# Another order in the middle of a hybrid mixer, and its second inverse transform as eight matmuls

## Chip, cores and metric

One Trainium2 chip, one of its cores. The metric is the time of one execution on the device in microseconds (us). Engines are named as the profile names them: PE is TensorE (PEld its weight loads), DVE is VectorE, ACT is ScalarE, POOL is GpSimd, SP is SyncE.

## What is computed

A two-layer encoder on 256 tokens of width 1024, in float32. Each layer is a SwiGLU block, a mixer, and another SwiGLU block; the mixer joins three branches and projects them by one 1024 x 1024 matrix.

```python
def hybrid_layer(x, ...):
    x = x + 0.5 * swiglu_ffn(rms_norm(x, ffn1_norm), ...)
    proj = rms_norm(x, mix_norm) @ w_in
    y_hy  = hyena_mixer(hy_in, ...)          # width 256
    y_mla = mla_mixer(mla_cq, mla_ckv, mla_kr, ...)   # 4 heads, width 512
    y_gla = gla_mixer(gla_q, gla_k, gla_v, ...)       # 4 heads, width 256
    x = x + jnp.concatenate([y_hy, y_mla, y_gla], axis=-1) @ w_out
    x = x + 0.5 * swiglu_ffn(rms_norm(x, ffn2_norm), ...)
    return x

def fft_long_conv(u, kern, skip):
    L = u.shape[1]
    U = jnp.fft.rfft(u, n=2 * L, axis=1)
    K = jnp.fft.rfft(kern, n=2 * L, axis=0)
    y = jnp.fft.irfft(U * K[None], n=2 * L, axis=1)[:, :L]
    return y + u * skip.astype(jnp.float32)

def hyena_mixer(u_proj, ...):
    u = centred_short_conv(u_proj, conv_w, conv_b).astype(jnp.float32)
    v, x1, x2 = jnp.split(u, HY_ORDER + 1, axis=-1)
    z = x1 * fft_long_conv(v, kern[:, 0], skip[0])
    y = x2 * fft_long_conv(z, kern[:, 1], skip[1])
    return rms_norm(y.astype(dtype), out_norm)
```

The attention branch (MLA) computes queries from a 256-wide latent and keys and values from a 128-wide one, turns 64 dimensions of each query and of one shared key by rotary angles, and takes a softmax over 256 keys. The gated linear attention branch (GLA) computes decayed scores between all pairs of tokens.

## The kernel before

**Tiling.** Tokens are 2 tiles (T) of 128. Products with weights run as three fp32r passes over a high and a low part: ACT copies the high part of a weight slot (L409, helper `hi`), DVE subtracts it for the low part (L681, helper `lo`), and PE runs L1036 to L1038 (helper `passes`). Weights stream through a ring of three slots of 1 MB, filled by SP. Products of activations with activations or small tables run in plain float32; each such matmul stands in the trace as two MATMUL records, so the four matmuls of one inverse transform are 8 records.

**Order.** Every engine runs its own list of instructions in the order of its block in the source, with semaphores between the lists; nothing else orders the work. A `wait_ge` on an engine holds all that follows on that engine.

**The Hyena branch.** Each of the two long convolutions (o = 0 and 1) is, in turn:
- `hy_dft` on PE (L1191): four float32 matmuls, the odd positions' half into one PSUM bank, the even half into another.
- `spectrum_odd` on ACT (L518): the odd half copied to SBUF; `join` on DVE (L840): even plus odd and even minus odd, into C, which holds the spectrum at both halves of the frequencies.
- `multiply` (L853) and `combine` (L863) on DVE: the complex product with the filter's spectrum. Both inputs of their four operations lie in SBUF; the result is Y, four parts of 256 columns.
- `fold` on DVE (L869): sums and differences of Y's halves, so that the inverse needs half as many matmuls; then it signals `h_y`.
- `hy_inverse` on PE (L1202): four float32 matmuls with the table `idft`; signals `h_inv`.
- `gated` on DVE (L874): times x1 or x2; signals `h_z`.

After o = 1, ACT sums squares (L640), POOL forms the reciprocal root (`rstd`, L321 to L323), and DVE scales the two tiles of 256 columns (L980 to L984), which signals `h_yy` for PE's transposes (`turn_group(l, 2, 0, ...)`, L1357).

**The GLA branch.** It runs eight levels. For each: `level_exp` on ACT (L522), `level_qk` on DVE (L801), `levels` on POOL (L339, four additions on line L350 that prepare the next level), `level_scores` on PE (L1178, line L1187, into banks 0 to 3), and `level_keep` on DVE (L807, a predicated copy, line L815). `level_scores(l, b)` waits until `level_keep(l, b - 1)` has emptied the banks (for b = 0: until ACT's copy to AD, L635). `level_exp(l, b)` waits for POOL's `levels(l, b - 1)` and DVE's `level_qk(l, b - 1)`.

**The attention branch.** Queries come out in bank 7 (rotary part, slot S_UQR) and banks 2 and 3; DVE forms the rotary products (L963 to L965, `a_qt`), POOL adds them (L379, `a_qr`), PE transposes (L1334), ACT copies out (L628, `a_qre`), and PE computes `scores` (L1209, lines L1212 and L1213): row block s = 0 into banks 4 and 5, s = 1 into banks 6 and 7. `hy_dft(l, 1, 6)` and `hy_inverse(l, 1, 6)` also use banks 6 and 7, so scores of s = 1 come after them. `score_max` on DVE (L817) and `probs` on ACT (L536) follow.

DVE's order after the second convolution, unchanged in source: `level_qk(2)`, `level_keep(0)`, `gated(1)`, `level_qk(3)`, `score_max(0)`, `level_keep(1)`, `level_qk(4)`.

## Time and profile before

| | |
|---|---|
| time of 3 runs | 1040.04 to 1040.89 us, median 1040.7 |
| profiled execution, its own time | 1040.12 us |
| its span, first to last instruction | 1038.1 us |
| granted TensorE clock, mean | 0.999 |
| PE busy | 1010.4 us, 97% of the span |
| DVE busy | 637.3 us, 61% |
| ACT busy | 485.4 us, 47% |
| POOL busy | 111.6 us, 11% |
| mean DMA rate | 169 GB/s |

Times inside the trace are counted from the first instruction; the layers are two copies of the same lists, and the mixer's middle lies near 255 to 330 us in layer 0 and 765 to 840 us in layer 1. Of a matmul the trace knows the start; its end is modelled. Where a row has a bracket, the engine sat idle for that long before it, and what ended the idle time is named. Line numbers are those of the kernel before.

### The profile page before, as it was taken

The numbers are of one execution on the slowest core, as the hardware profiler recorded it, in microseconds if no ns is written. First come the engines' busy times: TensorE is split into PE (matmuls) and PEld (weight loads), VectorE is DVE, ScalarE is ACT, GpSimd is POOL, SyncE is SP. The second block draws the span as 40 slices with busy tenths as digits, with TensorE's granted clock in tenths as the row PEclk, the third lists the DMA queues.
The fourth block names the chain that finished last, engine by engine and source line by source line (L and its number), as shares of the span: only waits on it lengthen the run. The fifth ranks groups of instructions, "written<-read, shape, count | busy, mean of one in ns | idle before, by whom it ended". The sixth has DMA issues, their size and how long they took to land.

```text
span 1038.1 us, 17426 instructions
## 1 busy us (share of the span) xinstructions
PE 1010.4 (97%) x7004; PEld 923.8 (89%) x7004; DVE 637.3 (61%) x738; ACT 485.4 (47%) x663; POOL 111.6 (11%) x160
## 2 busy tenths in 40 slices
PE   7999999999899999999999999999998999999997
PEld 6999999888778999999999999997886889999996
DVE  4655555676886655555566555557679765555555
ACT  6544434356654544343354443434566554434342
POOL 2000000150331100000020000003315220000001
PEclk9999999999999999999999999999999999999999
DMA  9565455444303554555555545552542245455551
GB/s 306 188 227 203 167 197 181 143 163 150 135 22 142 202 202 168 197 179 184 183 178 203 203 167 197 179 185 86 199 164 80 81 148 218 167 197 178 186 182 41
DMA packets 27084, 175.93 MB, mean 169 GB/s; under 512 B 3200, under 2 KB 3712, under 8 KB 6560
## 3 DMA queue, kind: packets, MB, share of 16 engines
q1 hardware_dynamic: 25744, 172.90, 46.5%
q0 software_dynamic: 720, 1.95, 0.7%
q8 instruction: 33, 0.54, 0.2%
q10 hardware_dynamic: 576, 0.45, 0.2%
q14 instruction: 11, 0.09, 0.0%
HBM read 174.58 MB, written 1.05 MB: 169 GB/s over the span
## 4 chain that ended last, share of the span: by engine, by line
issue 50%; PE 38%; POOL 9%; DVE 1%; DMA 1%; POOLq 1%; ACT 0%; SPq 0%; DVEq 0%; ACTq 0%
PE psum L1036 13%; PE psum L1037 13%; PE psum L1038 13%; POOL mixer_scratch L350 3%; POOL mixer_scratch L371 1%; POOL mixer_scratch L370 1%; DMA x<-in_x_dram 1%; POOL statistics L323 1%; POOL statistics L321 1%; POOL statistics L334 0%; POOL x_normed L375 0%; DVE x L727 0%; POOL statistics L337 0%; POOLq L226 0%; POOL mixer_scratch L372 0%
## 5 line engine op out<-in xcount | busy, mean ns | idle before, releaser
L681 DVE TENSOR_TENSOR w_low<-w_raw,w_high 128x2048 fp32r<-128x2048 f32 (+1 forms) x160 | 362.8, 2271 | 198.5 <-ACT w_high L409 198.5
L1036 PE MATMUL psum<-xT_high,w_high 128*128 128x256 f32 x1536 | 437.8, 285 | 1.7 <-DVE xT_low L691 1.6
L1037 PE MATMUL psum<-xT_low,w_high 128*128 128x256 f32 x1536 | 435.3, 283 | 0.0
L1038 PE MATMUL psum<-xT_high,w_low 128*128 128x256 f32 x1536 | 435.2, 283 | 0.0
L409 ACT ACTIVATE w_high<-w_raw 128x2048 fp32r<-128x2048 f32 (+1 forms) x160 | 299.1, 1874 | 99.1 <-PE psum L1038 96.3
L1036 PEld LDWEIGHTS psum<-xT_high,w_high 128*128 128x128 f32 x1536 | 295.2, 192 | 5.8 <-issue 4.0
L1037 PEld LDWEIGHTS psum<-xT_low,w_high 128*128 128x128 f32 x1536 | 295.4, 192 | 1.9 <-issue 0.5
L1038 PEld LDWEIGHTS psum<-xT_high,w_low 128*128 128x128 f32 x1536 | 295.4, 192 | 0.0
L457 ACT ACTIVATE silu_gate<-hidden 128x256 f32<-128x256 f32 x88 | 36.8, 418 | 298.9 <-DVE hidden L706 298.9
L1036 PE MATMUL psum<-w_high,hT_high 128*128 128x512 f32 (+1 forms) x360 | 140.0, 389 | 0.0
L1037 PE MATMUL psum<-w_low,hT_high 128*128 128x512 f32 (+1 forms) x360 | 139.7, 388 | 0.0
L1038 PE MATMUL psum<-w_high,hT_low 128*128 128x512 f32 (+1 forms) x360 | 139.2, 387 | 0.0
L1038 PEld LDWEIGHTS psum<-w_high,hT_low 128*128 128x128 f32 x360 | 67.6, 188 | 14.0
L1036 PEld LDWEIGHTS psum<-w_high,hT_high 128*128 128x128 f32 x360 | 67.8, 188 | 13.5 <-issue 0.8
L1037 PEld LDWEIGHTS psum<-w_low,hT_high 128*128 128x128 f32 x360 | 67.8, 188 | 12.3
L706 DVE TENSOR_TENSOR hidden<-psum,diag_rstd 128x256 f32<-128x256 f32 x88 | 37.2, 423 | 67.4 <-PE psum L1038 65.3
L334 POOL TENSOR_TENSOR statistics<-statistics,constants 128x1 f32<-128x1 f32 x14 | 9.1, 647 | 582.8 <-ACT x_normed L419 582.8
L710 DVE SCALAR_TENSOR_TENSOR hidden<-psum,silu_gate 128x256 f32<-128x256 f32 x88 | 37.3, 424 | 42.6 <-ACT silu_gate L457 42.6
L1036 PE MATMUL psum<-w_high,xT_high 128*128 128x512 f32 (+1 forms) x128 | 51.1, 400 | 0.0
L1038 PE MATMUL psum<-w_high,xT_low 128*128 128x512 f32 (+1 forms) x128 | 49.7, 388 | 0.0
L1037 PE MATMUL psum<-w_low,xT_high 128*128 128x512 f32 (+1 forms) x128 | 49.5, 387 | 0.0
L425 ACT ACTIVATE xT_high<-psum,par 128x256 fp32r<-128x256 f32 x64 | 25.1, 486 | 41.9 <-PE psum L1065 25.3
(180 smaller groups left out, 801.9 us busy)
## 6 DMA issues: line engine op xcount, KB each, us to landing
w_raw<-in_w_dram SPq DMA_DIRECT2D x160, 1024.0 KB, 4.8
w_raw<-in_w_dram SPq DMA_DIRECT2D x8, 256.0 KB, 7.9
x<-in_x_dram SPq DMA_DIRECT2D x2, 512.0 KB, 5.8
mixer_scratch<-in_fil_dram POOLq DMA_DIRECT2D x2, 512.0 KB, 6.6
out_dram<-x_normed SPq DMA_DIRECT2D x3, 256.0 KB, 2.1
mixer_scratch<-in_fil_dram POOLq DMA_DIRECT2D x2, 352.0 KB, 6.3
mixer_scratch<-in_fin_dram SPq DMA_DIRECT2D x1, 512.0 KB, 5.5
dft<-in_dft_dram SPq DMA_DIRECT2D x1, 256.0 KB, 5.1
```

The source lines that it names most:

```text
L321: link(l, e.tensor_tensor(b, a, cst[:, inv:inv + n], ALU.mult))
L323: e.tensor_tensor(b, b, cst[:, I_POW:I_POW + n], ALU.pow).then_inc(done.sem, 1)
L350: return e.tensor_tensor(to[:, :, side, :], to[:, :, side, :], o, ALU.add)
L409: e.activation(filled(WH[p], n), filled(raw[p], n), ACT.Copy).then_inc(s_hi.sem, 1)
L425: r = e.activation(by(XH[:, k, :]), halves(PS[:, bank, n * SEQ:(n + 1) * SEQ]), ACT.Copy, scale=par[:, col + k:col + k + 1])
L457: e.activation(sg[:, f, :], hid[:, f, :], ACT.Silu).then_inc(s_silu.sem, 1)
L681: e.tensor_tensor(filled(WL[p], n), filled(raw[p], n), filled(WH[p], n).bitcast(F32), ALU.subtract).then_inc(s_lo.sem, 1)
L706: e.tensor_tensor(hid[:, f, :], PS[:, 4 + 2 * pr + f, 0:SEQ], row, ALU.mult).then_inc(s_gn.sem, 1)
L710: e.scalar_tensor_tensor(out=hid[:, f, :], in0=PS[:, 4 + 2 * pr + f, SEQ:2 * SEQ], scalar=0.5 * float(D) ** 0.5, in1=sg[:, f, :], op0=ALU. ...
L1036: e.matmul(out, ah, bh, start=start, stop=False)
L1037: e.matmul(out, ah, bl, start=False, stop=False)
L1038: return e.matmul(out, al, bh, start=False, stop=stop)
```

## The change

- The inverse table gets two more blocks, the sine part with its sign turned (SBUF 4 to 6 blocks of 128 columns; the load from memory 512 to 768 columns).
- For o = 1, `combine` signals `h_y` itself, `fold` is left out, and `hy_inverse` runs eight matmuls on Y in place of four on C. For o = 0 nothing changes but the place: PE runs the inverse right after the S_UQN products, and DVE runs `combine` and `fold` right after `multiply`.
- DVE: `lo(S_UKV)` ahead of `level_qk(0)`, `gated(0)` ahead of the rotary products.
- ACT: the query copies ahead of the first key copy and `level_exp(1)`; `spectrum_odd(1)` ahead of the copy of the turned queries; the second key copy ahead of `hi(S_WO + 1)`.
- PE: `hy_dft(1)` ahead of the transposes of the rotary queries; two of the four heads of `scores(l, 1, ...)` ahead of `hy_inverse(1)`.
- The scaling of the Hyena output goes from DVE to ACT, behind `probs_turned(0)`.

```diff
--- before.py
+++ after.py
@@ -72,7 +72,7 @@
 NORMS = 3
 TURNS = 4
 
-LINKS = {"dve": 28, "pool": 49, "act": 2, "pool_end": 4}
+LINKS = {"dve": 27, "pool": 49, "act": 2, "pool_end": 4}
 
 
 class Mark:
@@ -122,7 +122,7 @@
         ident = cst[:, 0:P]
         st = sb("statistics", [P, NST + 1])
         dft = sb("dft", [P, T, 256])
-        idft = sb("inverse_dft", [P, 4, P])
+        idft = sb("inverse_dft", [P, 6, P])
         rope = sb("rope", [P, 2, T, DR])
         mask = sb("level_masks", [P, LEVELS - 1, P], U8)
         wg = sb("gate_weights", [P, 2, P])
@@ -292,7 +292,7 @@
                 e.sem_inc(landed[pos(n)].sem, 16)
             stream(1, FFN_SLOTS // RING // 2)
             for dst, src in ((dft[:].rearrange("p a b -> p (a b)"), dft_d[:, 0:512]),
-                             (idft[:].rearrange("p a b -> p (a b)"), dft_d[:, 512:1024]),
+                             (idft[:].rearrange("p a b -> p (a b)"), dft_d[:, 512:1280]),
                              (rope[:].rearrange("p a b c -> p (a b c)"), rope_d)):
                 e.dma_start(dst, src).then_inc(s_in.sem, 16)
             stream(FFN_SLOTS // RING // 2, DEPTH * SLOTS // RING)
@@ -615,21 +615,21 @@
                 natural(l, 3, 1, 4)
                 hi(l, S_WO)
                 values_out(1)
+                e.wait_ge(s_used.sem, used(l, S_UQN))
+                for n in range(2):
+                    copy(QN[:, 2 * n:2 * n + 2, :].rearrange("p a b -> p (a b)"), PS[:, 2 + n, :], a_qn)
                 e.wait_ge(a_km.sem, a_km.at(l))
                 copy(KN[:, 0:2, :].rearrange("p a b -> p (a b)"), PS[:, 4, :], a_kn)
                 level_exp(l, 1)
-                e.wait_ge(s_used.sem, used(l, S_UQN))
-                for n in range(2):
-                    copy(QN[:, 2 * n:2 * n + 2, :].rearrange("p a b -> p (a b)"), PS[:, 2 + n, :], a_qn)
                 e.wait_ge(a_vm.sem, a_vm.at(l))
                 copy(VM[:, 0, :], PS[:, 5, :], a_v)
                 copy(VM[:, 1, :], PS[:, 6, :], a_v)
+                spectrum_odd(l, 1, 7)
                 e.wait_ge(a_qtr.sem, a_qtr.at(l))
                 copy(QR.rearrange("p a b -> p (a b)"), PS[:, 2, :], a_qre)
-                spectrum_odd(l, 1, 7)
-                hi(l, S_WO + 1)
                 e.wait_ge(s_used.sem, used(l, S_UKV))
                 copy(KN[:, 2:4, :].rearrange("p a b -> p (a b)"), PS[:, 1, :], a_kn)
+                hi(l, S_WO + 1)
                 level_exp(l, 2)
                 e.wait_ge(g_ls.sem, g_ls.at(l, 1))
                 copy(AD.rearrange("p h t c -> p h (t c)"), PS[:, 0:4, 0:256], g_la)
@@ -642,6 +642,11 @@
                 probs(l, 0)
                 level_exp(l, 5)
                 probs_turned(l, 0)
+                e.wait_ge(h_r.sem, h_r.at(l))
+                for t in range(T):
+                    v = xn[:, t, 0:256]
+                    r = e.activation(v, v, ACT.Copy, scale=st[:, T_RH + t:T_RH + t + 1])
+                r.then_inc(h_yy.sem, 1)
                 level_exp(l, 6)
                 probs(l, 1)
                 turned_high(l, 2, 0, Y_BANKS[0], Y_TILES[0], C_GO, by_parity)
@@ -860,11 +865,15 @@
                 e.tensor_tensor(pairs(Y), pairs(C), both(KA[:]), ALU.mult)
                 link(l, e.tensor_tensor(pairs(TT), pairs(C), both(KI[:]), ALU.mult))
 
-            def combine(l):
+            def combine(l, o):
 
                 y, t = pairs(Y), pairs(TT)
                 e.tensor_tensor(y[:, :, 0, :], y[:, :, 0, :], t[:, :, 1, :], ALU.subtract)
-                link(l, e.tensor_tensor(y[:, :, 1, :], y[:, :, 1, :], t[:, :, 0, :], ALU.add))
+                r = e.tensor_tensor(y[:, :, 1, :], y[:, :, 1, :], t[:, :, 0, :], ALU.add)
+                if o:
+                    r.then_inc(h_y.sem, 1)
+                else:
+                    link(l, r)
 
             def fold(l):
 
@@ -946,11 +955,12 @@
                 lo(l, S_UQN)
                 join(l, 0, 0)
                 multiply(l, 0)
+                combine(l, 0)
+                fold(l)
                 lo(l, S_UQR)
+                lo(l, S_UKV)
                 level_qk(l, 0)
-                lo(l, S_UKV)
-                combine(l)
-                fold(l)
+                gated(l, 0, 0)
 
                 e.wait_ge(s_used.sem, used(l, S_UQR))
                 q = PS[:, 7, :].rearrange("p (t h d) -> p t h d", t=T, h=H)
@@ -963,13 +973,11 @@
                 e.tensor_tensor(t1, q, rp(0, 0, 64), ALU.mult)
                 e.tensor_tensor(t2[:, :, :, 0:32], q[:, :, :, 32:64], rp(1, 0, 32), ALU.mult)
                 e.tensor_tensor(t2[:, :, :, 32:64], q[:, :, :, 0:32], rp(1, 32, 64), ALU.mult).then_inc(a_qt.sem, 1)
-                gated(l, 0, 0)
                 lo(l, S_WO)
                 level_qk(l, 1)
                 join(l, 1, 6)
                 multiply(l, 1)
-                combine(l)
-                fold(l)
+                combine(l, 1)
                 level_qk(l, 2)
                 level_keep(l, 0)
                 gated(l, 1, 6)
@@ -977,11 +985,6 @@
                 score_max(l, 0)
                 level_keep(l, 1)
                 level_qk(l, 4)
-                e.wait_ge(h_r.sem, h_r.at(l))
-                for t in range(T):
-                    v = xn[:, t, 0:256]
-                    r = e.tensor_scalar(v, v, st[:, T_RH + t:T_RH + t + 1], None, ALU.mult)
-                r.then_inc(h_yy.sem, 1)
                 level_keep(l, 2)
                 level_qk(l, 5)
                 score_max(l, 1)
@@ -1203,7 +1206,12 @@
                 e.wait_ge(h_y.sem, h_y.at(l, o + 1))
                 for t in halves:
                     for part in range(2):
-                        r = e.matmul(PS[:, b, t * 256:(t + 1) * 256], idft[:, 2 * t + part, :], C[:, 2 * t + part, :], start=(part == 0), stop=(part == 1))
+                        u = PS[:, b, t * 256:(t + 1) * 256]
+                        if o == 0:
+                            r = e.matmul(u, idft[:, 2 * t + part, :], C[:, 2 * t + part, :], start=(part == 0), stop=(part == 1))
+                        else:
+                            e.matmul(u, idft[:, 2 * t + part, :], Y[:, part, :], start=(part == 0), stop=False)
+                            r = e.matmul(u, idft[:, 4 * t + part, :], Y[:, 2 + part, :], start=False, stop=(part == 1))
                 return r
 
             def scores(l, s, heads=range(H)):
@@ -1303,6 +1311,7 @@
                         r = passes(PS[:, 2 + h // 2, (h % 2) * SEQ:(h % 2 + 1) * SEQ], WH[p][:, k, h * P:(h + 1) * P], WL[p][:, k, h * P:(h + 1) * P],
                                    HH[:, k, :], HL[:, k, :], k == 0, k == 1)
                 r.then_inc(s_used.sem, 1)
+                hy_inverse(l, 0, 0).then_inc(h_inv.sem, 1)
                 e.wait_ge(s_lo.sem, s_lo.at(l, S_UQR + 1))
                 p = pos(S_UQR)
                 for t in range(T):
@@ -1324,18 +1333,18 @@
                     e.wait_ge(g_vr.sem, g_vr.at(l, t + 1))
                     r = passes(PS[:, 5 + t, :], KVH[:, t * P:(t + 1) * P], KVL[:, t * P:(t + 1) * P], WH[p][:, 1, :], WL[p][:, 1, :], True, True)
                 r.then_inc(a_vm.sem, 1)
-                hy_inverse(l, 0, 0).then_inc(h_inv.sem, 1)
                 e.wait_ge(h_oc.sem, h_oc.at(l, 1))
                 keys((2, 3)).then_inc(s_used.sem, 1)
+                e.wait_ge(a_qt.sem, a_qt.at(l))
+                e.wait_ge(a_v.sem, a_v.at(l, 2))
+                e.wait_ge(h_z.sem, h_z.at(l, 1))
+                hy_dft(l, 1, 6)
                 e.wait_ge(a_qr.sem, a_qr.at(l))
                 e.wait_ge(a_qn.sem, a_qn.at(l, 2))
                 for pair in range(2):
                     for t in range(T):
                         r = e.transpose(PS[:, 2, pair * SEQ + t * P:pair * SEQ + (t + 1) * P], xn[:, t, 768 + pair * P:768 + (pair + 1) * P], ident)
                 r.then_inc(a_qtr.sem, 1)
-                e.wait_ge(a_v.sem, a_v.at(l, 2))
-                e.wait_ge(h_z.sem, h_z.at(l, 1))
-                hy_dft(l, 1, 6)
                 e.wait_ge(s_kz.sem, 1)
                 e.wait_ge(a_qre.sem, a_qre.at(l))
                 scores(l, 0, (0, 1))
@@ -1344,13 +1353,15 @@
                 scores(l, 0, (2,))
                 level_scores(l, 0)
                 scores(l, 0, (3,)).then_inc(a_s.sem, 1)
+                e.wait_ge(h_oc.sem, h_oc.at(l, 2))
+                scores(l, 1, (2, 3))
                 hy_inverse(l, 1, 6).then_inc(h_inv.sem, 1)
                 level_scores(l, 1)
                 e.wait_ge(h_z.sem, h_z.at(l, 2))
-                scores(l, 1, (0, 1, 2))
+                scores(l, 1, (0,))
                 level_scores(l, 2)
                 turn_probs(l, 0)
-                scores(l, 1, (3,)).then_inc(a_s.sem, 1)
+                scores(l, 1, (1,)).then_inc(a_s.sem, 1)
                 level_scores(l, 3)
                 attend(l, 0)
                 e.wait_ge(h_yy.sem, h_yy.at(l))
@@ -1486,7 +1497,7 @@
     cst[:, I_G:I_EPS] = 1 / 64
     cst[:, I_EPS:I_POW] = EPS
     cst[:, I_POW:] = -0.5
-    dft = np.concatenate([dft, inv], 1)
+    dft = np.concatenate([dft, inv, -inv[:, 256:512]], 1)
     return {n: a.astype(f32) for n, a in dict(cst=cst, dft=dft, rope=rope, win=win, z=z[n].T, mask=mask).items()}
```

## Rows read from the trace of the kernel before

**Rows 1.** The page's first part: busy us (share of span) xinstructions

```profile
PE 1010.4 (97%) x7004; PEld 923.8 (89%) x7004; DVE 637.3 (61%) x738; ACT 485.4 (47%) x663; POOL 111.6 (11%) x160
```

**Rows 2.** Busy time by stretch: length, five engines' busy us (count), clock, DMA share, GB/s

```profile
271.00:287.00 16.00, 12.76 (x99) 9.92 (x97) 13.75 (x14) 9.85 (x15) 7.81 (x12) 1.00 0.20 75
...
781.00:797.00 16.00, 12.76 (x96) 9.94 (x98) 13.63 (x15) 10.04 (x16) 7.69 (x11) 1.00 0.22 80
```

**Rows 3.** Timeline of PE in layer 0: start, us, line, operation, count, idle before

```profile
267.39 0.28 PE L1036 MATMUL psum<-w_high,hT_high 128*128 128x256 f32 x1
...
269.43 0.28 PE L1038 MATMUL psum<-kvT_high,w_low 128*128 128x256 f32 x1
...
274.68 0.66 PE L1334 MATMUL psum<-constants,x_normed 128*128 128x128 f32 x4 [1.13 <-POOL x_normed L379]
275.18 1.89 PE L1194 MATMUL psum<-mixer_scratch,dft 128*128 128x256 f32 x8
...
279.18 0.73 PE L1187 MATMUL psum<-mixer_scratch 32*128 32x128 f32 x16 [0.38 <-ACT mixer_scratch L502]
...
281.14 0.73 PE L1187 MATMUL psum<-mixer_scratch 32*128 32x128 f32 x16 [0.17 <-ACT mixer_scratch L502]
...
284.48 1.99 PE L1206 MATMUL psum<-mixer_scratch,inverse_dft 128*128 128x256 f32 x8 [1.55 <-DVE mixer_scratch L872]
286.40 0.73 PE L1187 MATMUL psum<-mixer_scratch 32*128 32x128 f32 x16
...
290.65 0.73 PE L1187 MATMUL psum<-level_qk 32*128 32x128 f32 x16 [0.54 <-DVE mixer_scratch L815]
```

**Rows 4.** The inverse's line, both layers: ns min/median/max, starts, form

```profile
L1206 PE MATMUL psum<-mixer_scratch,inverse_dft x32: 378/379/483, 271.0 to 796.3; 128*128 128x256 f32 x32
```

**Rows 5.** Timeline of DVE in layer 0

```profile
273.49 3.28 DVE L681 TENSOR_TENSOR w_low<-w_raw,w_high 128x2048 fp32r<-128x2048 f32 x1
...
277.30 0.68 DVE L848 TENSOR_TENSOR mixer_scratch<-psum,mixer_scratch 128x512 f32<-128x512 f32 x1
...
279.75 1.22 DVE L861 TENSOR_TENSOR mixer_scratch<-mixer_scratch,filter_im 128x1024 f32<-128x1024 f32 x1
...
283.49 0.94 DVE L872 TENSOR_TENSOR mixer_scratch<-mixer_scratch 128x512 f32<-128x512 f32 x1
...
286.51 0.69 DVE L879 TENSOR_TENSOR x_normed<-psum,mixer_scratch 128x512 f32<-128x512 f32 x1 [0.26 <-PE psum L1206]
...
289.19 1.31 DVE L815 COPY_PREDICATED mixer_scratch<-level_masks,psum 128x1024 f32<-128x1024 uint8 x1
...
290.98 1.01 DVE L983 TENSOR_SCALAR x_normed<-x_normed,statistics 128x256 f32<-128x256 f32 x2
...
306.13 2.28 DVE L681 TENSOR_TENSOR w_low<-w_raw,w_high 128x2048 fp32r<-128x2048 f32 x1
```

**Rows 6.** Timeline of POOL in layer 0

```profile
271.34 2.07 POOL L350 TENSOR_TENSOR mixer_scratch<-mixer_scratch 128x128 f32<-128x128 f32 x4 [5.83 <-ACT silu_gate L533]
273.37 1.26 POOL L379 TENSOR_TENSOR x_normed<-mixer_scratch 128x512 f32<-128x512 f32 x1
...
279.81 1.48 POOL L350 TENSOR_TENSOR mixer_scratch<-mixer_scratch 128x128 f32<-128x128 f32 x1 [5.18 <-ACT silu_gate L533]
```

**Rows 7.** Timeline of ACT in layer 0

```profile
270.48 0.79 ACT L533 ACTIVATE silu_gate<-mixer_scratch 128x256 f32<-128x256 f32 x2
...
275.38 0.60 ACT L502 ACTIVATE mixer_scratch<-psum 128x512 f32<-128x512 f32 x1 [2.16 <-PE psum L1334]
...
276.74 1.90 ACT L409 ACTIVATE w_high<-w_raw 128x2048 fp32r<-128x2048 f32 x1
...
279.97 1.02 ACT L502 ACTIVATE mixer_scratch<-psum 128x1024 f32<-128x1024 f32 x1 [0.24 <-PE psum L1187]
...
295.05 0.72 ACT L533 ACTIVATE silu_gate<-mixer_scratch 128x256 f32<-128x256 f32 x2 [1.55 <-POOL mixer_scratch L350]
```

## The prediction

> **What bounds the kernel now.** The page comes first: PE is busy for 97% of the span [rows 1], so the end is set by PE's list, and only what PE does or waits for counts. The change touches one stretch per layer. The table by stretch shows where PE has room there: in the 16 us from 271 on it is busy for 12.76, and in layer 1 the same stretch gives the same 12.76 [rows 2]. The layers are copies, shifted by 510.2 us, so I work out one and double it. I next read PE's timeline, with the waits in brackets [rows 3], and then the other engines' timelines to see who is late [rows 5 to 7]. The brackets count from the modelled end of the matmul before. I count from the last issue, which adds about 0.16 us to each. Ahead of the second inverse PE then loses 1.29 us (rotary addition on POOL), 0.55 (at 279.18), 0.34 (at 281.14) and 1.71 (DVE's fold), 3.9 in all. Behind the inverse comes a chain that is not PE's: DVE's `gated` at 286.51, then without a gap to `level_keep(1)` at 289.19, which ends at 290.50, and only then `level_scores(2)` at 290.65 [rows 3, 5]. From `gated` also hang ACT's squares, POOL's root and POOL's next levels, which ACT's exponentials wait for until 295.05 [rows 7]. So the end of the second inverse is the clock of all that follows.
>
> **PE's added work.** The gap between records of a float32 matmul is (1.89 - 0.379) / 7 = 0.216 us: eight in 1.89, the last lasting 0.379 [rows 3, 4]. Eight more records are 1.73 us per layer, and all of it lies between the second inverse's start and `gated`. Before, `gated` starts 286.51 - 284.48 = 2.03 us behind the inverse's start [rows 3, 5]. After, it is 3.76.
>
> **DVE's removed work.** The fold's two operations cost 1.6 to 1.7 us (the second lasts 0.94 and ends at 284.43, and PE starts at 284.48) [rows 3, 5]. That makes `h_y` early. It gains time only if PE is there to use it.
>
> **The first inverse moved.** It now starts at 267.39. `h_y` must be there: `multiply` ended at about 262.9, and `combine` and `fold`, four operations of at most 0.94 [rows 5], end by 266.7. No wait. It pushes the S_UQR products and the first keys by 1.73: these are 18 matmuls from 267.39 to 269.43, 0.12 apart [rows 3], so the keys' end goes from 269.71 to 271.44. That is paid back when the inverse is absent from its old place, but ACT feels it: the first key copy now waits for 271.44, takes about 0.5, and `level_exp(1)`, before at 270.48 [rows 7], starts at 272.0 and ends at 272.8. The query copies, put ahead, fill the gap and cost nothing.
>
> **POOL's turn, and who is there first.** POOL's `levels(1)` ran at 271.34 in 2.07 us, while DVE had nothing to do, then the rotary addition in 1.26, done at 274.63 [rows 6]; PE's transposes waited for that. Now DVE forms the rotary products from 270.7 (S_UQR's end) to 272.05 and goes straight into `lo(S_WO)`. Undisturbed this lasts 2.28, as at 306.13 [rows 5], so until 274.3. POOL's first addition comes at 272.8, inside it. What happens then is to be seen elsewhere in the trace: at 279.81 one POOL addition took 1.48 us where four took 2.07 at 271.34 [rows 6]; it came 0.06 behind DVE's L861, with both inputs in SBUF, and ended 0.3 after that one's end at 280.97 [rows 5]. The other way round, `lo(S_WO)` took 3.28 where 2.28 is usual, having come 0.12 behind POOL's 1.26 [rows 5, 6]. So the later waits for the whole of the earlier. I let POOL wait until 274.3. The four additions then interleave with `level_qk(1)` (some 0.3 lost) and end at 276.5, and the rotary addition at 277.75: 3.1 us later than before. The bounds: without any blocking POOL would be done at 272.8 + 2.07 + 1.26 = 276.15 (1.5 late).
>
> The Trainium skill has this as a rule (SBUF - State Buffer, section "Who interferes with whom"): a DVE instruction with two SBUF inputs and a GpSimd instruction that reads SBUF exclude each other, and the first to issue holds the shared ports for its whole length. The longest block of POOL in this trace is behind a 1.22 us operation; if a hold ended at that length, POOL would be free some 1.0 us earlier than by the rule, and the sum below would be 2 us lower over both layers. The trace agrees with the rule as far as it goes.
>
> **PE up to the second inverse.** Keys and values now end earlier by their own list (273.4). `hy_dft(1)`, moved ahead of the transposes, waits for ACT's value copies, which stand behind `level_exp(1)`: to 274.0, a wait of 0.6, and ends at 275.7. Transposes wait to 277.8 (2.1). From their start to the end of ACT's copy of them is 275.98 - 274.68 = 1.30 [rows 3, 7], which `hy_dft(1)` used to cover and no longer does: scores start at 279.1, another wait of 0.8. With 8 records (1.72) `level_scores(-1)` stands at 280.85, without its old wait of 0.55. Its result goes to ACT's AD copy, which queues behind the copy of queries (from 278.5), of keys, `hi(S_WO + 1)` (1.9) and `level_exp(2)`: it starts at 282.0 and ends 1.02 later [rows 7], so `level_scores(0)` starts at 283.15, before at 281.14: 2.0 late. Then the level, the last head of s = 0, and the two heads taken forward (1.73): PE reaches the inverse at 283.15 + 0.65 + 0.97 + 1.73 = 286.5. `h_y` has been there since about 281.3, for `join` starts near 276 (before at 277.30 [rows 5]) and the fold is gone. The 1.71 us wait is gone, but what took its place is the moved heads and 2.0 us of new waits: the inverse starts 2.0 later than at 284.48.
>
> **The sum.** `gated` starts 2.0 + 1.73 = 3.75 later per layer. Behind it, DVE's chain to `level_keep(1)` is in source the same, and `score_max(0)` stands behind `gated` although its scores are long there, so DVE idles for some 5 us and then does it all late. PE has 1.73 us less to do behind the inverse, but that only lengthens its wait for `level_keep(1)`. The scaling taken from DVE (1.01 [rows 5]) can give at most 0.36: `level_keep(2)` cannot start before `level_scores(2)` ends, at 290.65 + 0.73 + 0.17 = 291.55, where it started at 291.91. On ACT the two scalings fall into the 1.55 us wait at 295.05 [rows 7]. Since ACT and POOL carry the same delay, I take 0.1 of it. Per layer 3.65, in all 7.3. The 128 KB more of table are loaded in the first block and hide there. The profiled execution took 1040.12 us itself, 0.6 below the median of 1040.7, within the spread of the three runs: 1040.1 + 7.3 = 1047.4. On the median it would be 1048.0.
>
> **Rivals.**
> *A. POOL isn't held (or little).* The rotary addition is there at 276.15, scores start at 277.5, the AD copy at 280.35 behind `level_exp(2)`, `level_scores(0)` at 281.5 (0.4 late), the inverse at 284.9. `gated` is 2.1 late: 2.0 x 2 = 4.0, 1044.1. For it: a small shift of ACT or DVE by 0.8 us would let POOL in first. Against it: both blocks seen, in [rows 5, 6].
> *B. Slack further on takes it up.* The exponentials and levels behind `gated` turn out shorter with DVE idle in between, and only the inverse's own 1.73 or less stays: 0.5 to 1 us a layer, about 1041.5. Against it: POOL, ACT and DVE all start from `gated`, and PE is busy for the rest of the stage.
> *C. Faster: the waits ahead of the inverse vanish.* PE without any wait would reach the inverse at 284.48 - 3.9 + 1.73 = 282.3, with `h_y` there; `gated` would start at 286.1, 0.44 earlier than before, and with the 0.36 of DVE's scaling 0.8 per layer: 1038.5. It decides at one point: the sum of the waits on POOL's rotary addition and the copies around it must stay under 0.8 us per layer; I get 4.2. It would need POOL's addition by 275.7.
> *D. The fold is not what is replaced,* that is, the compiled program has no longer PE work (records reused or overlapped): then 1.73 per layer less than forecast, 1043.9. The diff's eight calls with no sharing speak against it.
>
> **Chances.** Forecast 0.60; more collisions than forecast (each `join`, `multiply` pair behind POOL, up to 1 us a layer, 1049.4) 0.08; A 0.18; B 0.05; C 0.07; D 0.02. About 0.2%, or 2 us, is what a measurement of this kernel can tell from no change. Faster 0.08, same 0.06, slower 0.86. The range takes in the forecast, A, D and the collisions: 1043.2 to 1049.6.
>
> **What would show it.** Right: second inverse 16 records, start about 2 us later than 284.48; in front of it a wait at the transposes near 2 us for POOL L379, whose predecessor's first addition lasts about 1.7 us; DVE idle about 5 us before the second `gated`; PE idle about 2.3 us for `level_keep(1)` ahead of `level_scores(2)`; span 7 us longer, half per layer. Wrong: if POOL's four additions take 2.1 us (then A), or if `gated` comes within 0.5 us of 286.5 (then C), or if `gated` is late and the stage's end is not (then B).

## The result, and the profile after

| | before | after |
|---|---|---|
| median of the timed runs | 1040.63 us | 1050.68 us (1049.77 to 1052.82) |
| ratio to before, 95% interval | | 1.0101 [1.0085, 1.0117] |
| profiled execution, its own time | 1040.12 us | 1052.82 us |
| its span | 1038.1 us | 1050.7 us |
| mean granted TensorE clock | 0.999 | 0.992 |

The change made the kernel 10 us slower, 1.0%. The forecast was 1047.4 (range 1043.2 to 1049.6): right in sign, 3.3 us short, and 1.1 us outside the range. In the four runs the mean granted clock was 0.992, 0.994, 0.996 and 0.994 at 1052.82, 1050.56, 1049.77 and 1050.81 us, so the profiled execution is the slowest of them and 2.1 us above the median.

PE's timeline in layer 0 of the changed kernel (start, us, line, operation, count, idle before). Line numbers have moved: L1197 is `hy_dft`, L1346 the transposes, L1220 and L1221 `scores`, L1190 `level_scores`, L1211 the first inverse, L1213 and L1214 the second, L1228 `turn_probs`.

```profile
267.84 1.89 PE L1211 MATMUL psum<-mixer_scratch,inverse_dft 128*128 128x256 f32 x8
...
274.49 1.97 PE L1197 MATMUL psum<-mixer_scratch,dft 128*128 128x256 f32 x8 [0.51 <-issue]
278.28 0.66 PE L1346 MATMUL psum<-constants,x_normed 128*128 128x128 f32 x4 [1.82 <-POOL x_normed L379]
279.71 0.80 PE L1220 MATMUL psum<-mixer_scratch 128*128 128x256 f32 x2 [0.78 <-ACT mixer_scratch L502]
280.31 1.06 PE L1221 MATMUL psum<-mixer_scratch 128*128 128x256 f32 x2
...
283.01 0.95 PE L1190 MATMUL psum<-mixer_scratch 32*128 32x128 f32 x16
...
285.21 0.73 PE L1190 MATMUL psum<-mixer_scratch 32*128 32x128 f32 x16 [0.18 <-ACT mixer_scratch L502]
...
286.83 0.59 PE L1220 MATMUL psum<-mixer_scratch 128*128 128x256 f32 x2
...
288.56 0.59 PE L1213 MATMUL psum<-mixer_scratch,inverse_dft 128*128 128x256 f32 x2
...
292.10 0.73 PE L1190 MATMUL psum<-mixer_scratch 32*128 32x128 f32 x16
...
296.23 0.73 PE L1190 MATMUL psum<-level_qk 32*128 32x128 f32 x16 [2.15 <-DVE mixer_scratch L820]
296.89 1.73 PE L1228 MATMUL psum<-constants,mixer_scratch 128*128 128x128 f32 x8
298.42 1.06 PE L1220 MATMUL psum<-mixer_scratch 128*128 128x256 f32 x2
```

This execution reached the stage 0.45 us later than that of before: the first inverse starts at 267.84 where I put 267.39. Against [rows 3], the transposes start at 278.28, not 274.68, and wait 1.82 us for POOL. The second inverse starts at 288.56, not 284.48. `level_scores(2)` waits 2.15 us for DVE, not 0.54, and starts at 296.23, not 290.65. These are the waits that the forecast had, but the places are later than its own: 288.56 is 288.1 on the old count, for a forecast 286.5. What it did not have stands in the lines from 279.71 to 283.01: the two records of `scores` at 280.31 take 1.06 us, and the 16 of `level_scores` at 283.01 take 0.95, where 0.59 and 0.73 are the times later, at 286.83 and 292.10. The table by stretches of the changed kernel says why (window, length, busy us of the five engines, granted clock, DMA share, GB/s):

```profile
279.60:283.90 4.30, 4.19 (x25) 2.98 (x25) 2.83 (x4) 2.87 (x4) 1.28 (x2) 0.60 0.00 2
283.90:296.80 12.90, 10.44 (x88) 8.25 (x84) 5.73 (x7) 6.88 (x18) 5.32 (x13) 1.00 0.01 2
296.80:301.00 4.20, 4.20 (x35) 3.22 (x28) 2.71 (x3) 3.07 (x8) 2.50 (x6) 0.59 0.00 0
796.00:799.40 3.40, 3.28 (x8) 2.45 (x8) 2.64 (x4) 2.87 (x4) 0.45 (x1) 0.57 0.00 0
799.40:812.30 12.90, 10.55 (x85) 8.23 (x84) 5.40 (x8) 6.21 (x15) 5.50 (x13) 1.00 0.00 0
812.30:816.60 4.30, 4.19 (x32) 3.50 (x32) 2.41 (x3) 2.55 (x8) 3.14 (x6) 0.60 0.02 4
```

PE ran at a granted clock of 0.57 to 0.60 in four stretches of about 4 us, two in each layer. As the spells begin and end inside the stretches, this is its lower level, 1.2 GHz, for most of them and 2.4 GHz for the rest. The first spell begins behind the waits at 278.28 and 279.71, the second behind the wait at 296.23. Before, the stretches of [rows 2] stood at 1.00, and so did every stretch of 20 us from 0 to 1020 us.

DVE's timeline in the changed kernel, layer 0:

```profile
272.47 2.28 DVE L686 TENSOR_TENSOR w_low<-w_raw,w_high 128x2048 fp32r<-128x2048 f32 x1
274.67 1.00 DVE L810 TENSOR_TENSOR mixer_scratch<-mixer_scratch,silu_gate 128x512 f32<-128x512 f32 x1
...
292.21 0.69 DVE L888 TENSOR_TENSOR x_normed<-psum,mixer_scratch 128x512 f32<-128x512 f32 x1 [4.77 <-PE psum L1214]
```

POOL, same kernel and time:

```profile
273.29 1.84 POOL L350 TENSOR_TENSOR mixer_scratch<-mixer_scratch 128x128 f32<-128x128 f32 x1 [6.99 <-ACT silu_gate L533]
...
276.96 1.27 POOL L379 TENSOR_TENSOR x_normed<-mixer_scratch 128x512 f32<-128x512 f32 x1
```

`lo(S_WO)` holds from 272.47 to 274.75, and POOL's first addition, asked for at 273.29, lasts 1.84 us and ends at 275.13; all four took 3.72 us, where they took 2.07 before [rows 6]. DVE stands idle for 4.77 us before the second `gated`, where it was 0.26 [rows 5].

### The profile page after: what moved, and what is told of

Its sections match the earlier page's. It is cut to its first block, busy times and chain, and to the rows that moved or that the text cites. A ratio compares the mean times of both kernels' runs of the same rounds, so it can differ in the third digit from the quotient of the medians.

```text
span 1050.7 us, 17452 instructions
## 1 busy us (share of the span) xinstructions
PE 1019.5 (97%) x7020; PEld 930.8 (89%) x7020; DVE 632.3 (60%) x730; ACT 487.4 (46%) x667; POOL 111.5 (11%) x160
## 4 chain that ended last, share of the span: by engine, by line
issue 51%; PE 38%; POOL 9%; DVE 1%; DMA 1%; POOLq 1%; ACT 0%; SPq 0%; DVEq 0%; ACTq 0%
PE psum L1039 12%; PE psum L1040 12%; PE psum L1041 12%; POOL mixer_scratch L350 3%; POOL mixer_scratch L371 1%; POOL mixer_scratch L370 1%; DMA x<-in_x_dram 1%; POOL statistics L323 1%; POOL statistics L321 1%; POOL statistics L334 0%; POOL x_normed L375 0%; DVE x L732 0%; POOL statistics L337 0%; POOLq L226 0%; POOL mixer_scratch L372 0%
## 5 line engine op out<-in xcount | busy, mean ns | idle before, releaser
L502 ACT ACTIVATE mixer_scratch<-psum 128x512 f32<-128x512 f32 (+3 forms) x52 | 29.1, 598 | 34.0 <-PE psum L1190 7.6
```

The source lines that it names most:

```text
L502: r = e.activation(dst, src, ACT.Copy, **kw)
```

## The experiments

Every edit is to the kernel before or after, as named; the times are set against runs of the kernel before on the same chip.

| run | median us | ratio to before, 95% interval | mean clock of its runs |
|---|---|---|---|
| after | 1050.68 | 1.0101 [1.0085, 1.0117] | 0.992 to 0.996 |
| a1, before with eight matmuls | 1040.25 | 0.9999 [0.9989, 1.0009] | 0.998, 0.999 |
| a2, new order with fold | 1045.55 | 1.0048 [1.003, 1.0066] | 0.995 to 0.999 |
| a3, after with waits filled | 1047.13 | 1.0066 [1.0048, 1.0084] | 0.998, 0.999 |
| a4, after, `lo(S_WO)` late | 1045.21 | 1.0046 [1.0028, 1.0064] | 0.997 to 0.999 |
| b2, after, `score_max(0)` early | 1048.92 | 1.0081 [1.0064, 1.0098] | 0.995 to 0.998 |
| b3, after, front waits filled | 1048.55 | 1.0082 [1.0066, 1.0097] | 0.996, 0.997 |
| b4, a4 + b2 + filled | 1044.47 | 1.0041 [1.0025, 1.0056] | 0.998, 0.999 |
| c2, after, rotary addition first | 1044.27 | 1.0036 [1.0022, 1.0049] | 0.995 to 0.999 |
| d1, after, heads behind the inverse | 1043.51 | 1.0034 [1.002, 1.0047] | 0.997 to 0.999 |
| d2, after mended | 1039.05 | 0.9989 [0.9979, 0.9999] | 0.998, 0.999 |
| b1, a1 mended | 1039.46 | 0.9992 [0.9983, 1.0001] | 0.998, 0.999 |
| c1, a1 mended further | 1038.82 | 0.9983 [0.9974, 0.9993] | 0.998, 0.999 |

### Is it the matmuls or the order?

**a1.** The kernel before with the eight matmuls alone.

```diff
-                multiply(l, 1); combine(l); fold(l)
+                multiply(l, 1); combine(l, 1)          # signals h_y
-   r = e.matmul(u, idft[:, 2 * t + part, :], C[:, 2 * t + part, :], ...)
+   e.matmul(u, idft[:, 2 * t + part, :], Y[:, part, :], start=(part == 0), stop=False)
+   r = e.matmul(u, idft[:, 4 * t + part, :], Y[:, 2 + part, :], start=False, stop=(part == 1))
```

> The kernel before with the second inverse as eight matmuls on Y and nothing moved. My theory (the order, not the matmuls, costs the time): combine signals about 1.7 us earlier, at 282.8 us, when TensorE has just arrived (282.77); the inverse starts near 282.85 instead of 284.48, lasts 1.73 longer, and gated starts at 286.6 instead of 286.51. The time is within 0.5 us of the kernel before, 1040.6 to 1041.1, granted clock 0.999. Rival (the added matmuls on a TensorE that is 97% busy are what costs): 2 x 1.73 = 3.5 us more, 1044.1.

Measured: 1040.25 us, no change. The rival that had the added PE work as the cost is out for this order. In its trace (0.45 us later than before here too) the inverse starts at 283.22 without a wait, and `gated` comes at 286.97, so at 286.52 on the old count, where it was 286.51. PE's row of the inverse in a1's timeline, and DVE's row of `gated`:

```profile
283.22 0.69 PE L1213 MATMUL psum<-mixer_scratch,inverse_dft 128*128 128x256 f32 x2
```

```profile
286.97 0.69 DVE L883 TENSOR_TENSOR x_normed<-psum,mixer_scratch 128x512 f32<-128x512 f32 x1 [1.73 <-PE psum L1214]
```

The fold's time on DVE and the eight added records on PE pay for each other, to 0.01 us here.

**a2.** The changed kernel with `fold` and four matmuls back.

```diff
-                combine(l, 1)
+                combine(l)
+                fold(l)
```

> The changed kernel with the fold and four matmuls put back for the second inverse: the new order alone. My theory: TensorE still reaches the second inverse 2.0 us late, for the waits in front of it (rotary addition on GpSimd, copies on ScalarE) are the same; the fold is hidden behind them; the inverse is 1.73 shorter than in the changed kernel, so gated is about 2.0 us late: 4 us over both layers and 2 to 3 us from the lower granted clock as in the changed kernel: 1045 to 1047.5, clock 0.993 to 0.996. Rival (the matmuls cost, the order does not): 1041.

Measured: 1045.55 us, single runs from 1043.28 (clock 0.999) to 1046.33 (0.996). So the order alone costs some 3 us even in the run at full clock, and about 5 at the median. In this order the eight matmuls do cost: a3, below, has 1047.13 with them at such a clock, 3.9 us more, where 2 x 1.73 is 3.5. PE comes late, and nothing is won by an early `h_y`.

### What is the rest of the 10 us?

**a3.** The changed kernel with float32 matmuls on constants in PE's three waits (their result is overwritten and never read).

```diff
                 hy_dft(l, 1, 6)
+                fill(4, 0, 0)
...
                 r.then_inc(a_qtr.sem, 1)
+                fill(2, 0, 0)
...
                 scores(l, 1, (0,))
+                fill(5, 6, 256)
```

> The changed kernel with matmuls on constants put into TensorE's waits, so that it is never idle for long: four behind the second hy_dft, two behind the transposes of the queries, five behind the first head of the second row block (each 0.43 us at full clock; the result is overwritten). Theory (a lower granted clock after the long waits costs what my sum lacked): the records of the first scores go back from 0.86 to 0.43 us apart, mean clock 0.999, time 1047 to 1048.5. Rival (the clock is a side effect, the time lies in the chain of waits alone): 1050.7 or, where the fill outlasts a wait, up to 1 us more.

Measured: 1047.13 us, all runs within 0.3 us. PE has more to do and ends 3.5 us sooner. The clock theory holds, and this is the run that my sum describes: 0.66% of 1040.3 is 6.8 us, where I had 7.3. In its timeline of PE (L1219 is the fill, L1224 and L1225 `scores`) the scores no longer take the 1.06 us of 280.31:

```profile
276.20 1.89 PE L1219 MATMUL psum<-dft,inverse_dft 128*128 128x256 f32 x8
278.19 0.66 PE L1351 MATMUL psum<-constants,x_normed 128*128 128x128 f32 x4
278.68 1.03 PE L1219 MATMUL psum<-dft,inverse_dft 128*128 128x256 f32 x4
279.62 0.67 PE L1224 MATMUL psum<-mixer_scratch 128*128 128x256 f32 x2
280.13 0.60 PE L1225 MATMUL psum<-mixer_scratch 128*128 128x256 f32 x2
...
286.83 0.59 PE L1213 MATMUL psum<-mixer_scratch,inverse_dft 128*128 128x256 f32 x2
```

The inverse starts at 286.83. This execution was 0.35 us behind that of before at the stage's start (the first inverse at 267.74, where I put 267.39), so 286.5 on the old count: the forecast's figure.

**b3.** The same with the fill in front of the inverse alone.

```diff
                 hy_dft(l, 1, 6)
+                fill(4, 0, 0)
...
                 r.then_inc(a_qtr.sem, 1)
+                fill(2, 0, 0)
```

> a3 with the fill in front of the second inverse only (four and two matmuls), the wait of 2.15 us ahead of level_scores(2) left empty. If each of the two spells of lower clock has its own idle time in front of it, the first goes and the second stays: 1048.5 to 1049.5, clock near 0.996. If the second spell needs the first waits as well, both go and the time is that of a3, 1047.1, clock 0.998.

Measured: 1048.55 us, clock 0.996 or 0.997. By the time this is the first case, but its reason does not hold: the second spell does not come with every empty second wait. In the profiled execution layer 0 has no spell, and layer 1 has one behind the empty wait (the table by stretches, columns as above; granted clock 0.89 from 797 to 811 us):

```profile
287.00:301.00 14.00, 11.31 (x116) 9.03 (x114) 10.05 (x14) 8.52 (x30) 7.06 (x16) 1.00 0.01 1
...
797.00:811.00 14.00, 11.72 (x89) 9.67 (x83) 7.62 (x9) 6.44 (x20) 7.06 (x16) 0.89 0.00 1
```

The same lists, with the same wait of 2.15 us, gave a spell in layer 1 and none in layer 0 (PE's timeline):

```profile
294.13 0.73 PE L1190 MATMUL psum<-level_qk 32*128 32x128 f32 x16 [2.15 <-DVE mixer_scratch L820]
...
807.68 1.05 PE L1190 MATMUL psum<-level_qk 32*128 32x128 f32 x16 [2.15 <-DVE mixer_scratch L820]
```

So a spell isn't a fixed price of a wait. What decides it within one execution stays open.

### Which wait in front of the inverse?

**a4.** The changed kernel with `lo(S_WO)` in DVE's idle time.

```diff
-                lo(l, S_WO)
                 level_qk(l, 1)
...
                 level_keep(l, 0)
+                lo(l, S_WO)
                 gated(l, 1, 6)
```

> The changed kernel with VectorE's lo(S_WO) moved from the front of level_qk(1) to the long idle time ahead of the second gated, so that GpSimd's four additions of levels(1) do not stand behind a 2.28 us operation. Theory: the rotary addition is ready 1.4 to 1.6 us earlier (276.6 instead of 278.2), the transposes wait that much less, all behind them moves up: 3 us over both layers, 1047.5, and 1046 if the shorter waits let the clock stand. Rival (ScalarE's own queue, which ends in the AD copy, holds TensorE anyway): less than 0.5 us, 1050.2 or more.

Measured: 1045.21 us, a larger gain than expected. POOL's four additions took 2.56 us instead of 3.72, and the transposes started 2.61 us behind `hy_dft` (277.01 and 274.40) instead of 3.79. That is 1.2 us a layer, 2.4 of the 5.5 won. The rest I read as clock: in the stretch in which the changed kernel had its first spell, it is at 1.00 now (table by stretches, layer 0, then the four additions in POOL's timeline).

```profile
279.00:283.30 4.30, 4.13 (x45) 3.00 (x44) 3.32 (x5) 4.30 (x5) 1.79 (x4) 1.00 0.02 4
```

```profile
273.18 2.56 POOL L350 TENSOR_TENSOR mixer_scratch<-mixer_scratch 128x128 f32<-128x128 f32 x4 [6.99 <-ACT silu_gate L533]
```

**c2.** The changed kernel with two instructions of POOL changed in order.

```diff
-                levels(l, 1)
                 e.wait_ge(a_qt.sem, a_qt.at(l))
                 e.tensor_tensor(xn[:, :, 768:1024], ...).then_inc(a_qr.sem, 1)
+                levels(l, 1)
```

> The changed kernel with GpSimd's rotary addition ahead of levels(1) and nothing else. The addition is then asked for 0.05 us after lo(S_WO) has begun. If the later of the two waits for the whole of the earlier, it is done at 274.7 + 1.26 = 275.9 us (layer 0, as in the changed kernel's trace) instead of 278.2, the wait at the transposes falls from 1.82 to about 0.1, and 4 us go over both layers, with the clock 5: 1045.7 to 1046.7. If GpSimd comes first, the addition is done at 273.8 and lo(S_WO) lasts 3.3 us instead, the same for TensorE. If the queue on ScalarE behind it holds the stage, 1049.

Measured: 1044.27 us, 1.4 us below the expected range, and the plainest row on the block. POOL's timeline, and DVE's `lo(S_WO)` at the same time:

```profile
272.18 3.25 POOL L378 TENSOR_TENSOR x_normed<-mixer_scratch 128x512 f32<-128x512 f32 x1 [6.36 <-DVE mixer_scratch L975]
```

```profile
272.02 2.28 DVE L686 TENSOR_TENSOR w_low<-w_raw,w_high 128x2048 fp32r<-128x2048 f32 x1
```

Asked for 0.16 us behind a DVE operation of 2.28 us, POOL's addition of 1.26 lasted 3.25: 2.12 us until DVE's end at 274.30, and then 1.13, near its own time. The wait is for the whole of the other's operation, also where that is 2.28 us long. The Trainium skill (SBUF — State Buffer, "Who interferes with whom") calls the ports that DVE and GpSimd share an exclusive lock, and says of DVE's two-port modes that whoever issues first has them for the whole instruction; this trace agrees, here with a DVE operation that has two inputs in SBUF. PE's transposes go without any wait, since the addition is done at 275.4 and `hy_dft` ends later: they start 1.80 us behind `hy_dft` (275.84 and 274.04) instead of 3.79, 2.0 us a layer.

**d1.** The changed kernel with the two heads of `scores(l, 1, (2, 3))` behind the inverse.

```diff
-                scores(l, 1, (2, 3))
                 hy_inverse(l, 1, 6).then_inc(h_inv.sem, 1)
+                scores(l, 1, (2, 3))
```

> The changed kernel with the two heads of the second row block put back behind the second inverse. Theory: they stand for 1.73 us of the time at which the inverse starts; gated and all behind it come 1.73 us earlier per layer, and the wait of level_scores(2) is filled by them instead: 3.5 us over both layers and a part of the clock's, 1045 to 1047.2. Rival (the inverse is held by something else, or the heads are then in the way behind it): under 1 us, 1050.

Measured: 1043.51 us, below the range, as four of its six runs had a clock of 0.998 or 0.999 and 1043.3 to 1043.5 us; the two at 0.997 had 1045.2 and 1045.4. Against a3, at the same clock, that is 3.6 us, twice the 1.73 of the two heads. At that clock c2 is 4.3 us below a3 (its one run at 0.999 had 1042.84) and a4 2.7 to 2.9 (1044.26 and 1044.47): the heads and the addition held by `lo(S_WO)` are the two large costs of the new order. They add up: together they are 7.9 us, and d2, below, which has both moves and three more, is 8.1 us below a3. This run's profile also has the waits of 1.82 and 0.78 us in both layers, with a spell behind them in layer 0 (from 279.44, four pairs of records in 3.57 us) and none in layer 1 (from 792.96, in 1.89). The wait of `level_scores(2)` fell to 0.63 (PE's timeline, layers 0 and 1):

```profile
279.44 1.19 PE L1220 MATMUL psum<-mixer_scratch 128*128 128x256 f32 x2 [0.78 <-ACT mixer_scratch L502]
...
792.96 0.67 PE L1220 MATMUL psum<-mixer_scratch 128*128 128x256 f32 x2 [0.78 <-ACT mixer_scratch L502]
...
806.13 0.73 PE L1190 MATMUL psum<-level_qk 32*128 32x128 f32 x16 [0.63 <-DVE mixer_scratch L820]
```

### What hangs on `gated`?

**b2.** The changed kernel with `score_max(0)` ahead of `gated(1)`.

```diff
+                score_max(l, 0)
                 gated(l, 1, 6)
                 level_qk(l, 3)
-                score_max(l, 0)
```

> The changed kernel with score_max(0) ahead of gated(1) on VectorE, nothing else. Theory (the 4.8 us idle time of VectorE before gated costs what is queued behind it): level_keep(1) comes 1.37 us earlier behind gated, the wait of level_scores(2) falls from 2.15 to 0.8 us, the second spell of the lower clock gets shorter or goes: 2 to 3.5 us over both layers, 1047 to 1048.7. Rival (the chain from gated over ScalarE's squares and GpSimd's root and levels holds the stage): under 0.7 us, 1050.

Measured: 1048.92 us (1046.03 at clock 0.998 to 1050.18 at 0.995). The wait of `level_scores(2)` fell from 2.15 to 0.78 as expected, but the time went into waits for ACT's softmax: a new one of 0.73, and two that stand in a3 at 0.37 and 0.21 grew to 0.85 and 0.46 (PE's timeline, layer 0; L1228 is `turn_probs`, L1235 `attend`):

```profile
292.84 0.73 PE L1190 MATMUL psum<-level_qk 32*128 32x128 f32 x16 [0.78 <-DVE mixer_scratch L820]
294.29 1.09 PE L1228 MATMUL psum<-constants,mixer_scratch 128*128 128x128 f32 x8 [0.73 <-ACT mixer_scratch L542]
...
300.84 1.09 PE L1228 MATMUL psum<-constants,mixer_scratch 128*128 128x128 f32 x8 [0.85 <-ACT mixer_scratch L542]
...
303.05 2.05 PE L1235 MATMUL psum<-mixer_scratch 128*128 128x128 f32 x16 [0.46 <-ACT mixer_scratch L502]
```

From `level_scores(1)` (290.08) to the second `attend` (303.05) are 12.97 us; in a3 they are 13.20 (290.37 to 303.57). Of the 1.37 us, 0.23 come through. The chain from `gated` holds the stage. ACT starts the squares at 290.91 and runs without a gap through `level_exp(4)` and `probs(0)` to 294.24, and PE's new wait ends at 294.29; ACT's next exponentials wait 0.81 us, to 295.05, for POOL's levels, which follow the root without a gap (ACT's timeline):

```profile
290.91 0.42 ACT L640 ACTIVATE mixer_scratch<-x_normed 128x256 f32<-128x256 f32 x1 [5.44 <-DVE x_normed L888]
...
295.05 0.72 ACT L533 ACTIVATE silu_gate<-mixer_scratch 128x256 f32<-128x256 f32 x2 [0.81 <-POOL mixer_scratch L350]
```

The gain of this run is mostly clock.

**b4.** a4, b2 and a short fill (one matmul in each wait) together.

```diff
                 hy_dft(l, 1, 6)
+                fill(1, 0, 0)
...
                 r.then_inc(a_qtr.sem, 1)
+                fill(1, 0, 0)
...
                 scores(l, 1, (0,))
+                fill(1, 6, 256)
```

> The changed kernel with lo(S_WO) late (a4), score_max(0) ahead of gated(1) (b2), and one matmul on constants in each of the three waits to hold the clock. Theory: from a3's 1047.1 go 2.3 us for lo(S_WO) (2 x 1.17, as a4's transposes showed) and 1 to 2.7 for score_max: 1042.1 to 1043.8, clock 0.998. What is left over the kernel before is the inverse that is 1.73 longer with TensorE there for its start, the wait for the value copies and the AD copy's queue. Rival (POOL and ScalarE hold the stage behind gated): 1044.8.

Measured: 1044.47 us at 0.998 or 0.999, near the rival's 1044.8: from a3's 1047.13 go 2.7 us, and 2 x (1.18 + 0.23) is 2.8. This run and b2 say the same of `score_max`.

### Better versions

**b1.** a1 with `score_max(0)` ahead of `gated(1)`, POOL's root behind `levels(4)`, and the scaling on ACT.

```diff
# DVE
+                score_max(l, 0)
                 gated(l, 1, 6)
                 level_qk(l, 3)
-                score_max(l, 0)
...
-                    r = e.tensor_scalar(v, v, st[:, T_RH + t:T_RH + t + 1], None, ALU.mult)
# ACT
+                    r = e.activation(v, v, ACT.Copy, scale=st[:, T_RH + t:T_RH + t + 1])
# POOL: rstd(h_sq) one line down, behind levels(l, 4)
```

> a1 (the kernel before with eight matmuls) with what the idle time it opens on VectorE allows: score_max(0) ahead of gated(1), GpSimd's root of the Hyena squares behind levels(4), the scaling on ScalarE behind probs_turned(0). Theory: score_max's 1.37 us fit into the 1.73 us in which VectorE waits for the inverse; level_keep(1) comes 1.3 us earlier, level_scores(2) is then held by TensorE's own list and starts 0.5 earlier; 0.3 to 0.5 us per layer in all, 1039.3 to 1039.8. Rival (the exponentials and levels from gated on, over ScalarE and GpSimd, hold the later part anyway): 1040.1 to 1040.4.

Measured: 1039.46 us, 0.9992 [0.9983, 1.0001], 0.8 us below the kernel before and not quite clear of it.

**c1.** b1, and:

```diff
# POOL
-                levels(l, 1)
                 (rotary addition)
+                levels(l, 1)
# ACT
-                hi(l, S_WO + 1)
                 copy(KN[:, 2:4, :]...); level_exp(l, 2); copy(AD...)
+                hi(l, S_WO + 1)
```

> b1 with two more moves: GpSimd adds the rotary products ahead of levels(1), and ScalarE does the second key copy, level_exp(2) and the AD copy ahead of hi(S_WO + 1). Theory: the wait of 1.29 us ahead of TensorE's transposes and the 0.55 and 0.34 behind it go, but the second inverse then waits for VectorE (join at 276.7 instead of 277.3, combine done at 282.2), so only 0.6 us per layer come through: 1039.5 - 1.1 = 1038.3. Rival (VectorE's lo(S_WO) and level_qk(1) hold join where it is): 1039.4.

Measured: 1038.82 us, 0.9983 [0.9974, 0.9993], between theory and rival. This is faster than both kernels. In its timeline of PE the second inverse waits for DVE again, and starts at 282.21:

```profile
282.21 0.70 PE L1213 MATMUL psum<-mixer_scratch,inverse_dft 128*128 128x256 f32 x2 [1.26 <-DVE mixer_scratch L872]
```

**d2.** The changed kernel with the orders that the runs found.

```diff
# PE: scores(l, 1, (2, 3)) behind hy_inverse(l, 1, 6)
# POOL: rotary addition ahead of levels(l, 1); rstd(h_sq) behind levels(l, 4)
# DVE: score_max(l, 0) ahead of gated(l, 1, 6)
# ACT: hi(l, S_WO + 1) behind the AD copy
```

> The changed kernel with all that the runs found: rotary addition ahead of levels(1), heads behind the inverse, score_max(0) ahead of gated, root behind levels(4), AD copy ahead of hi(S_WO + 1). Theory: TensorE reaches the second inverse at 282.3 to 282.8 us with h_y there, as in c1 (282.2); time 1038.8 to 1040 and clock 0.998 or more. Rival (the first inverse's early place, which sends level_exp(1) 1.5 us later, keeps costing): 1041 to 1042.

Measured: 1039.05 us, 0.9989 [0.9979, 0.9999]. With five moves the 10 us are gone, and 1.3 more. In its timeline of PE the second inverse starts without a wait, at 282.56, where 282.3 to 282.8 were expected:

```profile
282.56 0.59 PE L1213 MATMUL psum<-mixer_scratch,inverse_dft 128*128 128x256 f32 x2
```

The rival, 1041 to 1042 for the first inverse's early place, did not come. Against c1, which has that inverse in its old place, 0.6 of 1040 us remain, less than these intervals can tell.

## Where the prediction was right, and where wrong

**The chain in front of the inverse: right.** The sum put the second inverse at 286.5; a3, which holds the clock, has it there. By parts: the addition behind `lo(S_WO)` at its first lasted 1.84 us (I had about 1.7), the transposes waited 1.82 + 0.16 (2.1), the scores 0.78 + 0.16 (0.8), the inverse has 16 records.

**The heads taken forward: right.** d1 shows them at 1.8 us a layer, against 1.73.

**The blocked addition: right.** The whole of 2.28 us holds, as c2 shows. What moving `lo(S_WO)` gives in front of the transposes was 1.2 us a layer rather than the 1.4 to 1.6 expected of a4. I read the rest as `level_qk(1)`, which DVE starts at 273.13 there, 0.05 us ahead of POOL's four additions: they took 2.56 us, not 2.07.

**The fold and the eight matmuls: right.** They balance in the old order (a1).

**DVE's queue behind `gated`: right as to what waits, too strong as to what it costs.** DVE idled 4.77 us and did `score_max(0)` late. But b2 and b4 give 0.23 us a layer for it; it is the squares, the root and the levels that hold the stage, which the prediction's first paragraph had named beside DVE's chain.

**The sum: short by a whole term. This is the step that failed.** It took every duration at the granted clock of 1.00, that of [rows 2], and put the cost of the clock at nothing without a reason, while it had waits of 0.6, 2.1, 0.8 and 2.3 us on PE in each layer. The forecast's own 7.3 us came as 6.8 (a3). The other 3.5 are spells at the lower clock, two per layer in the profiled execution, and fewer where the mean clock is higher. Neither the terms, nor the rivals, nor the range had it: "more collisions" went up to 1049.4 by another cause. The range missed by 1.1 us for that: a3, without the spells, is inside it. In the profiled execution the four pairs of records from 279.71 to 283.01 took 3.30 us for 1.89 at full clock (d1's layer 1, 792.96 to 794.85), and `turn_probs` to `attend` 4.17 (296.89 to 301.06) for 2.54 in a3 (295.19 to 297.73): 1.4 + 1.6 us in a layer, 6 in all, of which the kernel's end shows 1052.8 - 1047.1 = 5.7.

**Rivals.** A (POOL not held), C (faster) and D (no longer PE work) are refuted by the profile after. B (slack takes it up) did not happen either, beyond a trace: in a3 the second `gated` starts 3.6 us late in layer 0 (290.48, 290.13 on the old count, for 286.51), and 3.35 us reach the next layer (their first `hy_dft`, at 257.55 and 771.10, are 513.55 us apart, where the layers were 510.2). So 0.3 us a layer was made up, where I took 0.1; that is about the difference of 7.3 and 6.8.

## What to carry to other kernels

An operation taken off an engine gives time only where its consumer is waiting for it, and work that fills one engine's wait ahead of a step on which the others depend delays all of them: the two heads of scores cost their full length, 1.8 us a layer, though PE was idle before and after. Before moving a long operation of DVE with two inputs in SBUF, look who on POOL asks in that time: in each case seen here it waited to the end, for 1.22 and for 2.28 us operations. And where a sum adds idle time to PE, price a lower clock behind it as a case of its own, with the starts of PE's records up to twice as far apart for some microseconds (0.86 us from pair to pair at 281.16, 0.43 at 287.26, in the changed kernel).

## What the runs showed of the hardware

The granted clock fell in the middle of a stage in which no single wait of PE was longer than 2.15 us. In front of the first spell PE had stood still for 1.82 us and, 1.4 us later, for 0.78; in front of the second for 2.15 (the waits in the first fence). The largest wait of the kernel before in this stage is 1.55 us [rows 3], and no spell stood behind it. The Trainium skill says in general that a hardware block sets the clock by how busy TensorE has lately been (TensorE: Matmul & The Clock Gate, "What's actually happening"); the runs agree as far as filling the waits kept the clock up (a3). b3's layer 0 kept it with the second wait empty, and d1's layer 1 with the first two, so the length of these waits alone doesn't decide it.

The same kernel gave different clocks from run to run: d1's runs fall into 1043.3 to 1043.5 us at 0.998 or 0.999 and 1045.2 to 1045.4 at 0.997, and a2's spread over 3 us. The kernels with PE's waits filled or shortened by several moves (a3, b4, d2) spread less, 0.998 or 0.999 in all runs; so the mean clock is to be read beside each time.
